# All working tiles of a one-core decoder layer moved by 128 bytes against the weight buffers

## The chip, the cores and the metric

The kernel runs on one core of one Trainium2 chip. The time is the device time of one execution in microseconds (us); smaller is better. Three runs of the kernel before gave 1163.86, 1164.48 and 1166.04 us, median 1164.48.

## The reference

One layer of a decoder trunk on a sequence of 512 tokens with 1024 channels in float32: a half-step FFN, a mixer of two gated linear attention branches, a second half-step FFN, and a last RMSNorm. Shift, scale and gate of each sub-layer come from a vector c.

```python
mod = (cond @ w_ada[l] + b_ada[l]).reshape(b_, N_SUB, 3, d)
h = modulate(rms_norm(x, norm_gains[l, 0]), mod[:, 0, 0], mod[:, 0, 1])
x = x + 0.5 * mod[:, 0, 2][:, None, :] * swiglu(h, ffn1_w_in[l], ffn1_w_down[l])
h = modulate(rms_norm(x, norm_gains[l, 1]), mod[:, 1, 0], mod[:, 1, 1])
proj = h @ w_in_mix[l]
...
merged = (jax.nn.sigmoid(r_hg) * (y_hg @ w_up_hg[l])
          + jax.nn.sigmoid(r_gla) * (y_gla @ w_up_gla[l]))
x = x + mod[:, 1, 2][:, None, :] * (merged @ w_out[l])
h = modulate(rms_norm(x, norm_gains[l, 2]), mod[:, 2, 0], mod[:, 2, 1])
x = x + 0.5 * mod[:, 2, 2][:, None, :] * swiglu(h, ffn2_w_in[l], ffn2_w_down[l])
```

The FFNs have 2816 inner channels; the attention branches (HGRN2 and GLA) have four heads each and are computed in chunks of 64 tokens.

## The kernel before

**Precision.** A float32 product is made of three matmuls in fp32r, which takes one pass: both operands are split into a high part (rounded to fp32r) and a low part (the rest), and high x high, high x low and low x high are added in PSUM (`three`, lines 640 to 645, and the loop in `product`, line 891). So every activation tile exists twice, as in HH and HL, UH and UL, TH and TL, MH and ML, and so does every piece of weights, as WH and WL.

**Weights.** They come as units of 256 output columns and up to eight blocks of 128 rows. SyncE's queue loads a unit into RAW0 or RAW1, ScalarE rounds it into WH0 or WH1 (line 1277), VectorE subtracts (WL0 or WL1, line 1817), and TensorE uses it; two buffers take turns. In the FFNs' input projections, the pairs from the third on are computed by a scheme with seven block products in place of eight (Strassen's): `swiglu_sevens` loops over the pairs, twice 1512 matmuls of 256 columns, all at line 891, from 80 to 257 us and from 851 to 1024 us. VectorE and ScalarE make the combined weights by way of SW, and the combined activations TH and TL once. The other units are matmuls of 512 columns (`unit`, `unit_x`), or of 256 (`first_units`, `last_unit`, and some of the first down projection). In the value units (`unit_v`, lines 688 to 690) the roles are swapped: 128 tokens of HH or HL are the weights and 256 columns of WH or WL move. In the low-rank unit the weights are 16 columns wide. The last unit of the first down projection and of the output projection uses LWH and LWL, which lie in the arena.

**Order.** All engines run programs that were written out by hand with semaphores. The change touches none of them.

**Memory.** SBUF tensors are allocated one after the other, each partition from its start: X, RAW0, RAW1, WH0, WH1, WL0, WL1, S, small constants, and at the end one tensor `arena` of 34928 elements (139712 bytes) of each partition. WH0 lies at 49280, WL0 at 65664; every slice of 128 columns of these starts at 128 modulo 512. All other working tiles are laid over the arena (`place`): HH, HL, UH, UL, TH, TL, MH, ML, LWH, LWL, the attention's tiles, the staging buffers of VectorE and ScalarE, and the destinations of the adaLN weights' loads. Each offset in `place`, and each slice of 128, 256 or 512 tokens in them, is a multiple of 512 bytes, with few small exceptions in the attention. So the moving operands of all wide matmuls start at one address modulo 512, which is that of `base`:

```python
arena = sb("arena", [P, (ARENA + 2 * H_BYTES) // 4 + 112])
base = arena_offset(nc, arena)

def place(name, shape, offset, dt=F32):
    return nc.alloc_sbuf_tensor_at(name, shape, dt, offset=base + offset)
```

The tensor `arena` starts at 88960, which is 384 modulo 512. It has 448 bytes (112 elements) more than its tiles need. `arena_offset` gives the first address from there that is 192 modulo 512: 89280.

Of the kernel before, what the change touches and what calls it, by code (L numbers as in the profile page):

```python
# [23 lines left out]
def trunk_program(nc, x, c, w_ada, b_ada, norm_gains, ffn1_w_in, ffn1_w_down, w_in_mix, w_gk_up, b_gk_up,  # L24
# [48 lines left out]
    with ctx:  # L73
# [35 lines left out]
        ARENA = 106496  # L109
# [4 lines that stand above are left out]
# [2424 lines left out]
def arena_offset(nc, arena):  # L2538

    size = arena.shape[1] * 4  # L2540
    start = (nc.sbuf_base - size) // 32 * 32
    return start + (192 - start) % 512


# [21 lines left out]
```

How the kernel before makes its waits and increments, by code:

```python
        @block.sync  # L405
# [1 line left out]
            def load(n, nslot, dst_cols, src, wait=None):  # L407
                if wait is not None:
                    sp.wait_ge(unit_lo, wait)
                sp.dma_start(dst_cols, src).then_inc(raw_in[nslot], 16)
# [36 lines left out]
            load_pair(0)
            with sp.Fori(1, NP - 1) as i:
                load_pair(i)
            for j in range(11):
                n = N_F1DOWN + j
                kb0, nk = ((0, 8), (8, 8), (16, FB - 16))[j % 3]
                load(n, slot(n), raw(n, nk), cols(ffn1_w_down[0], j // 3 * CW, kb0, nk), n - 1)
                if j == 6:
                    sp.wait_ge(unit_done, 2 * NP)
                    sp.dma_start(LRAW[0][:, :, :], cols(ffn1_w_down[0], 3 * CW, 16, FB - 16)).then_inc(last_in, 16)
            wm = w_in_mix[0]
# [5 lines left out]
            for pair in range(DB // 2):  # L467
                n = N_END + 3 * pair
                load(n, slot(n), raw(n), cols(wm, RHG + CW * pair), n - 1)
                load(n + 1, slot(n + 1), raw(n + 1), cols(wm, RGLA + CW * pair), n)
                up = raw(n + 2)
                sp.wait_ge(unit_lo, n + 1)
                sp.dma_start(up[:, 0:4, :], cols(w_up_hg[0], CW * pair, 0, 4)).then_inc(raw_in[slot(n)], 16)
                sp.dma_start(up[:, 4:8, :], cols(w_up_gla[0], CW * pair, 0, 4)).then_inc(raw_in[slot(n)], 16)
# [14 lines left out]
                sp.dma_start(out[0, t * P:(t + 1) * P, cs], OUTT[:, t, cs]).then_inc(out_dma, 16)  # L489
            sp.wait_ge(fin_a, 2)
            store(0, slice(0, D))
```

## Time and profile before

| | |
|---|---|
| runs, us | 1163.86, 1164.48, 1166.04 |
| profiled execution, us | 1160.54 |
| its span, first to last instruction, us | 1158.5 |
| mean granted TensorE clock | 0.995 of full |
| TensorE busy | 1131.1 us, 98% |
| weight loads busy (they overlap) | 1011.1 us, 87% |
| VectorE, ScalarE, GpSimd busy | 67%, 44%, 9% |
| chain that ended last | TensorE 86%, VectorE 7%, ScalarE 4% |

A matmul's duration in the profile is longer than its distance from the next one, since they are pipelined. Where TensorE never idles, the number of matmuls in a stretch and the distance between their starts say more than the busy share.

### The profile page before, as it was taken

How to read it: one execution, taken by the hardware profiler on the slowest of the kernel's cores; microseconds unless marked ns; L12 is line 12 of the kernel's file. 1: busy time of each engine (PE TensorE's matmuls, PEld its weight loads, DVE VectorE, ACT ScalarE, POOL GpSimd, SP SyncE). 2: the span in 40 equal slices, each digit the busy share in tenths (PEclk: the TensorE clock that was granted, in tenths of full speed). 3: DMA queues.
4: the chain of work that ended last, by engine and by line, in shares of the span. 5: the costliest groups of instructions: out<-in, count | busy, mean ns of one | idle time of the engine just before them, and what ended most of it. 6: DMA issues, size and time to landing. Idle time of an engine off the chain costs nothing.

```text
span 1158.5 us, 18518 instructions
## 1 busy us (share of the span) xinstructions
PE 1131.1 (98%) x7359; PEld 1011.1 (87%) x7359; DVE 778.3 (67%) x1061; ACT 507.2 (44%) x647; POOL 109.4 (9%) x172
## 2 busy tenths in 40 slices
PE   6999999999999999999999999999999999999997
PEld 5789999998889997877887888878999999988887
DVE  4789888867887656567763456855868888863322
ACT  6445544454212465555464321234445545442322
POOL 2000000002221032120210024300000000000000
PEclk9899999999999999999999999999999999999999
DMA  9424333337886222121312457642223333332211
GB/s 351 160 83 135 109 109 107 99 108 246 282 284 217 73 74 73 40 73 42 105 37 74 163 174 245 192 145 73 74 73 109 109 109 109 109 123 85 93 64 73
DMA packets 115799, 144.83 MB, mean 125 GB/s; under 512 B 4420, under 2 KB 103136, under 8 KB 115744
## 3 DMA queue, kind: packets, MB, share of 16 engines
q1 hardware_dynamic: 106800, 113.32, 30.1%
q0 software_dynamic: 8704, 30.68, 7.7%
q8 instruction: 37, 0.61, 0.2%
q14 instruction: 18, 0.15, 0.0%
q10 hardware_dynamic: 240, 0.08, 0.0%
HBM read 140.65 MB, written 2.10 MB: 123 GB/s over the span
## 4 chain that ended last, share of the span: by engine, by line
PE 86%; DVE 7%; ACT 4%; issue 1%; DMA 1%; SPq 0%; DVEq 0%; ACTq 0%
PE PS L891 29%; PE PS L643 16%; PE PS L645 16%; PE PS L644 16%; PE PS L1066 1%; PE PS L688 1%; PE PS L690 1%; PE PS L689 1%; DVE ACC L1919 1%; DMA ADA<-in_w_ada_dram 1%; DVE ACC_FIRSTa L1930 1%; PE PS L970 1%; ACT WH L1277 1%; PE PS L805 1%; DVE ACC_FIRSTb L1930 1%
## 5 line engine op out<-in xcount | busy, mean ns | idle before, releaser
L1817 DVE TENSOR_TENSOR WL<-RAW,WH 128x2048 fp32r<-128x2048 f32 (+2 forms) x55 | 120.5, 2190 | 137.5 <-ACT WH L1277 137.3
L643 PE MATMUL PS<-HH,WH 128*128 128x512 f32 (+2 forms) x488 | 186.6, 382 | 4.3 <-DVE HL L1845 3.2
L1277 ACT ACTIVATE WH<-RAW 128x2048 fp32r<-128x2048 f32 (+2 forms) x55 | 100.5, 1828 | 189.8 <-PE PS L645 181.1
L645 PE MATMUL PS<-HH,WL 128*128 128x512 f32 (+2 forms) x488 | 178.3, 365 | 0.0
L644 PE MATMUL PS<-HL,WH 128*128 128x512 f32 (+2 forms) x488 | 177.8, 364 | 0.0
L891 PE MATMUL PS<-HH,WH 128*128 128x256 f32 x576 | 160.5, 279 | 0.7 <-DVE WL L2107 0.6
L891 PE MATMUL PS<-HH,WL 128*128 128x256 f32 x576 | 159.9, 278 | 0.0
L891 PE MATMUL PS<-HL,WH 128*128 128x256 f32 x576 | 159.9, 278 | 0.0
L643 PE MATMUL PS<-UH,WH 128*128 128x512 f32 (+1 forms) x416 | 146.7, 353 | 0.0
L645 PE MATMUL PS<-UH,WL 128*128 128x512 f32 (+1 forms) x416 | 146.3, 352 | 0.0
L644 PE MATMUL PS<-UL,WH 128*128 128x512 f32 (+1 forms) x416 | 145.6, 350 | 0.0
L891 PE MATMUL PS<-TH,WH 128*128 128x256 f32 x432 | 120.1, 278 | 0.0
L891 PE MATMUL PS<-TH,WL 128*128 128x256 f32 x432 | 119.9, 278 | 0.0
L891 PE MATMUL PS<-TL,WH 128*128 128x256 f32 x432 | 119.9, 278 | 0.0
L643 PEld LDWEIGHTS PS<-HH,WH 128*128 128x128 f32 (+1 forms) x488 | 91.6, 188 | 24.2 <-issue 5.5
L891 PEld LDWEIGHTS PS<-HH,WH 128*128 128x128 f32 x576 | 108.1, 188 | 1.4 <-DVE WL L2107 1.0
L2101 DVE TENSOR_TENSOR WL<-SW,WH 128x1024 fp32r<-128x1024 f32 x72 | 88.1, 1224 | 31.2 <-ACT WH L1460 30.9
L891 PEld LDWEIGHTS PS<-HH,WL 128*128 128x128 f32 x576 | 108.2, 188 | 0.0
L891 PEld LDWEIGHTS PS<-HL,WH 128*128 128x128 f32 x576 | 108.0, 187 | 0.1
L645 PEld LDWEIGHTS PS<-HH,WL 128*128 128x128 f32 (+1 forms) x488 | 91.5, 187 | 16.7
L644 PEld LDWEIGHTS PS<-HL,WH 128*128 128x128 f32 (+1 forms) x488 | 91.8, 188 | 15.2 <-issue 1.3
L1460 ACT ACTIVATE WH<-SW 128x1024 fp32r<-128x1024 f32 x72 | 76.3, 1060 | 63.0 <-PE PS L891 60.1
(345 smaller groups left out, 2219.6 us busy)
## 6 DMA issues: line engine op xcount, KB each, us to landing
RAW<-in_ffn_w_in_dram SPq DMA_DIRECT2D x42, 1024.0 KB, 5.1
ADAW<-in_w_ada_dram POOLq DMA_DIRECT2D x56, 512.0 KB, 6.0
RAW<-in_w_in_mix_dram SPq DMA_DIRECT2D x22, 1024.0 KB, 5.2
RAW<-in_ffn_w_down_dram SPq DMA_DIRECT2D x16, 1024.0 KB, 5.1
ADA<-in_w_ada_dram SPq DMA_DIRECT2D x16, 512.0 KB, 10.5
RAW<-in_ffn_w_down_dram SPq DMA_DIRECT2D x7, 768.0 KB, 5.7
RAW<-in_w_out_dram SPq DMA_DIRECT2D x3, 1024.0 KB, 5.8
XST<-in_x_dram SPq DMA_DIRECT2D x4, 512.0 KB, 5.3
```

The source lines that it names most:

```text
L643: mm(ps, whi, ahi, start=start, stop=False)
L644: mm(ps, whi, alo, start=False, stop=False)
L645: return mm(ps, wlo, ahi, start=False, stop=stop)
L688: mm(ps, HH[:, k, tok], whi[:, k, :], start=k == 0, stop=False)
L689: mm(ps, HL[:, k, tok], whi[:, k, :], start=False, stop=False)
L690: ins = mm(ps, HH[:, k, tok], wlo[:, k, :], start=False, stop=k == DB - 1)
L891: ins = mm(PS[:, bank, ROW], wt, at_tokens[:, k, :], start=start and k == 0 and j == 0, stop=k == 3 and j == 2, skip_group_check=True)
L1277: A(WH[slot(n)][:, 0:size], RAW[slot(n)][:, 0:size], ACT.Copy).then_inc(unit_hi, 1)
L1460: A(WH[tile][:, 8 * P * (1 - j):8 * P * (2 - j)], SW[:, 2 * j:2 * j + 2, :].rearrange("p s c -> p (s c)"), ACT.Copy).then_inc(op_hi, 1)
L1817: V.tensor_tensor(WL[s][:, 0:size], RAW[s][:, 0:size], WH[s][:, 0:size].bitcast(F32), ALU.subtract)\
L1930: V.scalar_tensor_tensor(ACC_FIRST[half][:, :], w, COND[:, k:k + 1], ACC_FIRST[half][:, :], ALU.mult, ALU.add)\
L2101: V.tensor_tensor(WL[tile][:, w], SW[:, 2 * j:2 * j + 2, :].rearrange("p s c -> p (s c)"), WH[tile][:, w].bitcast(F32), ALU.subtract).then ...
```

## The change

The address of the arena's tiles modulo 512 bytes becomes 320 in place of 192. The first such address from 88960 is 89408, so that every tile that `place` lays out lies 128 bytes higher, and the last ends where the tensor `arena` ends. X, RAW, WH, WL, S and the constants stay. The instructions and their order on each engine are the same.

```diff
@@ -2539,7 +2539,7 @@
 
     size = arena.shape[1] * 4
     start = (nc.sbuf_base - size) // 32 * 32
-    return start + (192 - start) % 512
+    return start + (320 - start) % 512
```

## Rows read from the trace of the kernel before

**Rows 1.** The page's parts 1 and 4, of the whole span
```profile
PE 1131.1 (98%) x7359; PEld 1011.1 (87%) x7359; DVE 778.3 (67%) x1061; ACT 507.2 (44%) x647; POOL 109.4 (9%) x172
...
PE 86%; DVE 7%; ACT 4%; issue 1%; DMA 1%; SPq 0%; DVEq 0%; ACTq 0%
```

**Rows 2.** The chain that ended last in order of time: start us, us, what
```profile
95.94 162.41 PE PS L891 x1380
...
862.32 162.49 PE PS L891 x1428
```

**Rows 3.** Busy time by stretch of us from the start; the header names the columns
```profile
core 0: us, PE busy (x) PEld busy (x) DVE busy (x) ACT busy (x) POOL busy (x), PEclk, DMA share, GB/s
44.00:50.00 6.00, 5.49 (x15) 4.37 (x16) 4.90 (x7) 2.97 (x4) 0.00 (x0) 0.59 0.18 62
92.00:105.00 13.00, 12.88 (x114) 12.71 (x113) 12.01 (x17) 7.38 (x12) 0.00 (x0) 1.00 0.48 160
105.00:257.00 152.00, 152.00 (x1293) 152.00 (x1292) 123.94 (x160) 76.31 (x101) 0.00 (x0) 1.00 0.32 104
696.00:767.00 71.00, 71.00 (x308) 57.67 (x308) 47.82 (x53) 18.56 (x13) 23.18 (x35) 1.00 0.71 216
868.00:1024.00 156.00, 156.00 (x1378) 155.91 (x1377) 132.06 (x171) 80.56 (x108) 0.00 (x0) 1.00 0.33 108
```

**Rows 4.** Groups, 106:256, then 870:1023 us; columns: xcount | busy us, mean ns | idle
```profile
L891 PE MATMUL PS<-HH,WH 128*128 128x256 f32 x245 | 68.6, 280 | 0.0
...
L891 PE MATMUL PS<-HH,WH 128*128 128x256 f32 x259 | 71.5, 276 | 0.0
```

**Rows 5.** Timeline of PE, 512 columns, two runs' first and last: start us, us, ...
```profile
747.64 0.40 PE L645 MATMUL PS<-YHh,WL 128*128 128x512 f32 x1
...
750.91 0.40 PE L644 MATMUL PS<-YLh,WH 128*128 128x512 f32 x1
...
1041.13 0.39 PE L643 MATMUL PS<-UH,WH 128*128 128x512 f32 x1
...
1043.19 0.39 PE L643 MATMUL PS<-UH,WH 128*128 128x512 f32 x1
```

**Rows 6.** Timeline of PE, first and last of 26 on LWH and LWL
```profile
791.83 0.28 PE L643 MATMUL PS<-MH,LWH 128*128 128x256 f32 x1
...
794.83 0.28 PE L644 MATMUL PS<-ML,LWH 128*128 128x256 f32 x1
```

**Rows 7.** Groups, whole span; the last row, of line 690, has ns min/median/max
```profile
L643 PE MATMUL PS<-HH,WH 128*128 128x512 f32 x352 | 146.0, 415 | 0.9 <-DVE HL L1953 0.7
...
L643 PE MATMUL PS<-UH,WH 128*128 128x512 f32 x264 | 104.0, 394 | 0.0
...
L643 PE MATMUL PS<-UH,WH 128*128 128x256 f32 x152 | 42.8, 281 | 0.0
...
L644 PE MATMUL PS<-HL,WH 128*128 128x256 f32 x128 | 35.8, 279 | 0.0
...
L645 PE MATMUL PS<-HH,WL 128*16 128x512 f32 x8 | 3.2, 395 | 0.0
...
L690 PE MATMUL PS<-WL,HH x128: 276/281/283, 416.3 to 598.2; 128*128 128x256 f32 x128
```

**Rows 8.** Timeline of all engines about the wait at 397 us
```profile
397.27 0.28 PE L645 MATMUL PS<-HH,WL 128*128 128x256 f32 x1
...
398.28 0.19 PEld L643 LDWEIGHTS PS<-HH,WH 128*128 128x128 f32 x1 [0.93 <-DVE HL L1845]
```

**Rows 9.** Groups by line and form, 397.42:398.26 us, which only this matmul and one before reach
```profile
L645 PE MATMUL PS<-HH,WL 128*128 128x256 f32 x1 | 0.3, 279 | 0.0
```

**Rows 10.** Timeline of PE at the start of the first FFN
```profile
45.93 0.63 PE L643 MATMUL PS<-HH,WH 128*128 128x512 f32 x1
...
48.49 0.59 PE L643 MATMUL PS<-HH,WH 128*128 128x512 f32 x1
```

**Rows 11.** Timeline of PE where the second loop enters the lower level
```profile
868.15 0.36 PE L891 MATMUL PS<-HH,WH 128*128 128x256 f32 x1
```

## The prediction, made before the changed kernel ran

> **What bounds the kernel.** I read the page first, then the groups of matmuls by line and shape, then stretches of the timeline at the resolution of single matmuls. The page says that TensorE is busy for 98% of the span and holds 86% of the chain that ended last [rows 1]; VectorE holds 7% of that chain and the DMAs 1%. Two pieces of the chain are unbroken runs of 1380 and 1428 matmuls of the seven-product loops, 162 us each [rows 2]. So the time is the sum of the distances from one matmul's start to the next one's, and a change that moves no instruction can only act through these distances. The change moves none: it moves addresses. The profiled execution took 1160.54 us around a span of 1158.5; the median of the runs is 1164.48, so 4 us lie between them, and I put my differences on the median.
>
> **What the distances are.** They are not set by the shape alone. In the first seven-product loop (105 to 257 us) 1293 matmuls of 256 columns fill 152.0 us, 117.6 ns each; in the second (868 to 1024 us) 1378 of them fill 156.0 us, 113.2 ns each [rows 3]. The code, the operands' tiles and the granted clock (1.00) are the same. Their durations differ in the same way, 280 ns in the first loop, 276 in the second [rows 4]. The matmuls of 512 columns also have two levels: 9 steps in 2.06 us from 1041.13 (228.9 ns) and 14 steps in 3.27 us from 747.64 (233.6 ns) [rows 5]. I call them the lower and the upper level; they are 4.4 to 4.7 ns apart in both shapes. A third value stands where weights and moving operand both lie in the arena: 25 steps of matmuls on LWH and LWL take 3.00 us, 120.0 ns each [rows 6]. There the two operands start at the same address modulo 512, everywhere else in the main work they start 64 bytes apart, the moving one above; in the value units (lines 688 to 690) HH and HL are the weights and WH and WL move, so the moving one is 64 below.
>
> **What the change does.** The arena goes up by 128 bytes as a whole, from 89,280 to 89,408. (1) Instructions, waits, DMAs and their order: none added, removed or moved, 0 us. (2) Operands that both lie in the arena keep their distance: LWH and LWL, the scores, the VectorE and ScalarE work within it, 0 us. (3) Both old and new start are multiples of 64 and not of 256. The DMAs into the arena keep their size and number; all of them together hold 1% of the chain, some 12 us [rows 1], of which a tenth either way would be 1.2 us, and I take 0 since the pieces keep their size. (4) What is left is the distance between the operands in the wide matmuls, 64 bytes before and 192 now (in the value units 64 below becomes 192 below). With weights of 128 columns no row has this distance, so its price is bounded from both sides.
>
> The counts for these bounds: of the 3024 matmuls at line 891, 1492 lie in the two stretches at the lower level (1378 and 114, [rows 3]), so about 1530 are at the upper. Other matmuls of 256 columns and mean 279 to 281 ns, upper level, are 456 on UH and UL, 384 on HH and HL at lines 643 to 645, and 384 of the value units, of which I take 320 as upper since their shortest is 276 and their median 281 [rows 7]. That makes 2690 upper and 1490 lower. Of 512 columns there are 1056 on HH, HL and 792 on UH, UL [rows 7] and 336 more on the M and Y tiles (three times the 48 and 64 that the code's loops give), 2184 in all; the 308 from 696 to 767 us [rows 3] lie about the run of 233.6 ns and are taken as upper, some 1870 are lower.
>
> Lower bound of the time: all go to the lower level, 2690 x 4.4 ns = 11.8 us and 310 x 4.6 ns = 1.4 us less, 1164.5 - 13.2 = 1151.3. Upper bound: all go to the upper level, 1490 x 4.4 ns = 6.6 us and 1870 x 4.6 ns = 8.6 us more, 1179.7. The price of equal placement is as high: 2690 x 2.4 ns and 1490 x 6.7 ns would be 16.4 us, 1180.9, the wide matmuls not counted.
>
> **Which value I take: zero.** Three things speak against a dependence on the distance of 64 against 192. First, a matmul keeps its level when no weights load beside it. The last one before a wait, from 397.27 us, has the next load only at 398.28 [rows 8], and lasts 279 ns [rows 9], exactly like its neighbours in that upper stretch. If the extra time of a level were a collision of the moving stream with the next weights, this one should have been rid of it. Second, the value units have the moving operand 64 below the weights in place of 64 above, and show the same pair, 276 as the least and 281 as the median [rows 7]. A sign that changes nothing makes it likely that a size that stays clear of zero changes nothing. Third, in the low-rank unit the weights are 16 columns wide and step by 64 bytes with each k, so their distance runs through 64, 0 and on to 192 at k = 6; its matmuls of 512 columns mean 395 ns on line 645 [rows 7], within the two levels of the others, though their loads are short. Against all this stands only the 120.0 ns at distance zero. The second loop enters the lower level about 868.15, where one matmul lasts 0.36 us in place of 0.28 [rows 11], and no operand's placement changes there, so I take the levels as a matter of how the streams fall in step after an interruption. That can fall otherwise in another execution: the profiled execution and the median are 4 us apart with the same addresses, about what one loop's change of level is worth (1293 x 4.4 ns = 5.7 us).
>
> Of the two operands' reads the page's rows say nothing. The Trainium skill ("TensorE: Matmul & The Clock Gate", on the drain phase of a matmul; "SBUF — State Buffer", "SBUF: two separate sides") has moving data and weights read through two independent ports, and says that engines meet only at a port that VectorE and GpSimd share. By that rule the change is worth nothing at any distance. The trace agrees for 64 above and 64 below, and disagrees at distance zero, where 118 has become 120 ns; the sum by the rule is the same 0 as mine.
>
> **The rivals.**
> A, faster: the nearness of 64 bytes is what lets the upper level in, and three times the distance shuts it out. For it: at zero the distance is longest (120.0), at 64 shorter, so farther may be shorter still. Against it: the matmul without a load, and the second loop, which holds the lower level for 156 us at a distance of 64. If the first loop alone turns, 5.7 us go: 1158.8; if all do, 1151.3.
> B, slower: at 192 bytes the two streams meet in the middle of a matmul where at 64 they did not, and the second loop, with all that is now lower, loses its level. The place is 868 to 1024 us and the 512-column units on either side; the price 6.1 us for the loop (1378 x 4.4), 1170.6, and up to 1179.7 with the rest. It decides as soon as more than 520 matmuls turn (520 x 4.4 ns = 2.3 us, 0.2%). For it: the lower level holds in only about half the work, so it is easily lost; against it, the same three things as for my forecast.
> C, much faster: everything above the bare stream goes. At the lower of the clock's two levels, 1.2 GHz (granted 0.59 over 44 to 50 us, [rows 3]), six matmuls of 512 columns take 2.56 us, 427 ns each [rows 10]; half of it is 213.5 ns against 229 at 2.4 GHz, and 106.7 for 256 columns. That would be 15.5 x 1870 + 20 x 310 ns for the wide ones and 11 x 2690 + 6.5 x 1490 ns for the others, some 74 us, 1090. Nothing but arithmetic is for it.
> D, it does not do what it says: ruled out by the allocation, since 448 spare bytes of the arena are exactly what the new start needs, and every tile in it moves alike.
>
> **How the numbers follow.** No dependence on the distance: 0.45, and the median then lies within 1161 to 1168, since it can still fall in step otherwise. A 0.28, B 0.25, C 0.02. A measurement tells about 0.2% (2.3 us) from nothing. Of the 0.45 I give 0.37 to the same time and 0.04 to either side, so faster 0.34, same 0.37, slower 0.29. The time is that of the likeliest case, 1164.0, half a microsecond below the median because the profiled execution was 4 us below it. The range takes in A nearly to its end and B to its end, 1152 to 1179, and leaves C out.
>
> **What would show it.** Right: the second loop again near 113 ns a matmul and the first near 118, or the two changed about with the same sum; LWH still 120; the value units with least 276. A is right if no stretch of 256 columns shows 279 or more. B is right if the second loop's mean duration is 279 or more and fewer than 1340 matmuls lie in 156 us. I am wrong at the root if a duration appears that before does not have, below 276 or above 283 ns for 256 columns outside LWH, or outside 388 to 398 ns for 512, in an unbroken run: then the distance enters the price itself and not the level.

## The result and the profile after

The changed kernel takes 1170.32 us, the median of 4 runs (1169.38 to 1172.32), against 1164.65 of the kernel before (1163.86 to 1166.04, 4 runs). The ratio is 1.0042 with a 95% interval of 1.0025 to 1.006: slower by 0.4%, 5.7 us. The profiled execution is one of the four, 1169.64 us, with a span of 1167.6. Of all runs reported here one, of the kernel with the arena at 160, took 1878.43 us at a granted clock of 0.56; it is left out.

The page's parts 1 and 4 of the changed kernel, the same lines as [rows 1]:
```profile
PE 1140.5 (98%) x7359; PEld 1014.1 (87%) x7359; DVE 779.5 (67%) x1061; ACT 508.1 (44%) x647; POOL 110.1 (9%) x172
...
PE 88%; DVE 6%; ACT 3%; issue 1%; DMA 1%; SPq 0%; DVEq 0%; ACTq 0%
```
The counts are those of before; TensorE is busy for 9.4 us more in a span that is 9.1 longer. In the chain of waits the first loop's piece is as long as in [rows 2], the second's 5.8 us longer (start us, us, what):
```profile
94.47 162.77 PE PS L891 x1380
...
864.33 168.26 PE PS L891 x1428
```
The stretches of [rows 3], the columns as there:
```profile
44.00:50.00 6.00, 5.28 (x23) 4.31 (x24) 5.11 (x7) 3.19 (x4) 0.00 (x0) 1.00 0.30 104
92.00:105.00 13.00, 12.88 (x110) 12.71 (x110) 11.22 (x17) 8.09 (x12) 0.00 (x0) 1.00 0.39 130
105.00:257.00 152.00, 152.00 (x1293) 152.00 (x1292) 123.40 (x159) 75.24 (x100) 0.00 (x0) 1.00 0.32 104
696.00:767.00 71.00, 71.00 (x310) 57.34 (x309) 49.61 (x52) 19.10 (x14) 23.74 (x35) 1.00 0.68 208
868.00:1024.00 156.00, 156.00 (x1329) 155.91 (x1328) 131.12 (x170) 79.25 (x105) 0.00 (x0) 1.00 0.32 105
```
The first loop still holds 1293 matmuls in 152 us. The second holds 1329 in place of 1378 in 156 us: it is at the upper level now, and the granted clock is 1.00 in both. The groups of the two loops over the same stretches as in [rows 4], first and second, say the same by their durations:
```profile
L891 PE MATMUL PS<-HH,WH 128*128 128x256 f32 x244 | 68.6, 281 | 0.0
...
L891 PE MATMUL PS<-HH,WH 128*128 128x256 f32 x251 | 70.5, 281 | 0.0
```
The matmuls of 512 columns, where [rows 5] had 228.9 ns in the last down-projection, in the timeline of TensorE (the first and the last of 23):
```profile
1047.83 0.39 PE L643 MATMUL PS<-UH,WH 128*128 128x512 f32 x1
...
1052.97 0.39 PE L644 MATMUL PS<-UL,WH 128*128 128x512 f32 x1
```
That is 22 steps in 5.14 us, 233.6 ns each. LWH and LWL, which keep their distance of zero, keep their price of [rows 6] (first and last of 36):
```profile
794.76 0.28 PE L643 MATMUL PS<-MH,LWH 128*128 128x256 f32 x1
...
798.95 0.28 PE L645 MATMUL PS<-MH,LWL 128*128 128x256 f32 x1
```
35 steps in 4.19 us are 119.7 ns. Last, the groups that answer to [rows 7], of the whole span:
```profile
L643 PE MATMUL PS<-UH,WH 128*128 128x512 f32 x264 | 105.1, 398 | 0.0
...
L643 PE MATMUL PS<-UH,WH 128*128 128x256 f32 x152 | 42.9, 282 | 0.0
...
L690 PE MATMUL PS<-WL,HH x128: 277/279/283, 416.0 to 598.4; 128*128 128x256 f32 x128
```
The 512-column group is 4 ns longer; the 256-column ones stay within the old pair of durations.

A trace gives the start of every matmul, so the span can be added up by shape. The table shows the sum of the distances to the next start in us and, for the steady ones, the mean in ns; "interrupted" are distances of over 266 ns, in waits or at the low clock of the opening (for 256 columns, over 138 ns, not shown). The loops are counted from their thirteenth matmul; "other 256" leaves LWH and LWL out. The columns before and after come from the profiles above; the two on the right are the first pair of experiments, the same two programs again.

| | before | after | before again | after again |
|---|---|---|---|---|
| profiled execution | 1160.54 | 1169.64 | 1166.83 | 1172.98 |
| 512 columns, steady | 2116: 486.4 (229.9) | 2127: 496.2 (233.3) | 2115: 486.0 (229.8) | 2128: 496.4 (233.3) |
| 512, interrupted | 92: 39.6 | 81: 33.0 | 93: 39.9 | 80: 32.9 |
| first loop | 175.6 (117.4) | 175.7 (117.4) | 175.9 (117.6) | 176.0 (117.7) |
| second loop | 170.1 (113.7) | 175.5 (117.3) | 175.8 (117.5) | 175.3 (117.2) |
| other 256, steady | 143.3 (117.5) | 141.2 (116.1) | 143.3 (117.5) | 142.0 (116.7) |

The first pair's 9.1 us come from two large parts: the steady 512-column matmuls, (233.3 - 229.9) x 2127 = 7.2 us, and the second loop, 5.4 us. Against them, "other 256" is 2.1 us shorter, and by its 200th matmul (at 52 us) the kernel after is 1.8 us ahead. The medians are only 5.7 us apart: the profiled execution of before was 3.3 us below the fastest of its four runs.

### The profile page after: what moved, and what is told of

The parts are those of the page before. It is cut to its first block, busy times and chain, and to the rows that moved or that the text cites. A ratio compares the mean times of both kernels' runs of the same rounds, so it can differ in the third digit from the quotient of the medians.

```text
span 1167.6 us, 18518 instructions
## 1 busy us (share of the span) xinstructions
PE 1140.5 (98%) x7359; PEld 1014.1 (87%) x7359; DVE 779.5 (67%) x1061; ACT 508.1 (44%) x647; POOL 110.1 (9%) x172
## 4 chain that ended last, share of the span: by engine, by line
PE 88%; DVE 6%; ACT 3%; issue 1%; DMA 1%; SPq 0%; DVEq 0%; ACTq 0%
PE PS L891 29%; PE PS L643 17%; PE PS L645 16%; PE PS L644 16%; PE PS L1066 1%; PE PS L688 1%; PE PS L690 1%; PE PS L689 1%; DVE ACC L1919 1%; DMA ADA<-in_w_ada_dram 1%; DVE ACC_FIRSTa L1930 1%; PE PS L970 1%; ACT WH L1277 1%; PE PS L805 1%; PE PS L976 1%
```

## The experiments

After the result I had two theories. **Distance**: the price of a matmul depends on how far the moving operand's start lies from the weights', 64 bytes against 192, and the second loop's change of level is part of it. **Own address**: it depends on where the arena itself lies modulo 512 (320 against 192). A third was that the whole loss is the second loop and **chance**. Sixteen runs follow, of fourteen new kernels and the two again. All times are medians in us, with the range and the number of runs. Five chips were used; each ratio is to runs of the kernel before on the same chip in the same hour, so it is the ratios that compare across kernels.

**The two programs again.** No edit.

> The kernel before, unchanged, for a second profile. Theory D (distance): the time of the wide matmuls hangs on how far the moving operand starts from the weights, modulo 512. Then the 512-column runs stand at 229 ns again as they did in the first profile (outside 696 to 767 us), whatever the 256-column loops do. Theory C (chance): both shapes fall into a level by chance after each interruption. Then the 512-column runs change their level against the first profile in some stretches of hundreds of matmuls. Both expect 1164 to 1166 us; for the two seven-product loops I expect that the level can differ from the first profile, 113 or 118 ns.

> The changed kernel, for a second profile. Theory D (distance): 512-column runs at 233.4 ns throughout, as in its first profile, 1169 to 1172 us. Theory C (chance): runs at 229 ns appear in some stretches, and the time scatters toward 1165.

Before again 1166.61 (1164.38 to 1167.26, 10 runs), ratio to the other runs of before 1.0004 (0.9994 to 1.0014). After again 1172.91 (1171.89 to 1173.6, 4), 1.0055 (1.0037 to 1.0073). The stretches from 868 us and the opening, of before again:
```profile
44.00:50.00 6.00, 5.29 (x15) 4.15 (x15) 5.17 (x7) 3.23 (x4) 0.00 (x0) 0.57 0.21 73
868.00:1024.00 156.00, 156.00 (x1329) 155.90 (x1328) 129.68 (x168) 78.12 (x104) 0.00 (x0) 1.00 0.32 105
```
and of after again:
```profile
44.00:50.00 6.00, 4.56 (x21) 3.48 (x22) 5.15 (x9) 2.84 (x5) 0.00 (x0) 1.00 0.54 175
868.00:1024.00 156.00, 155.89 (x1329) 155.72 (x1328) 131.83 (x172) 79.09 (x106) 0.00 (x0) 1.00 0.33 108
```
The second loop holds 1329 matmuls in both: with the old addresses, too, it can run at the upper level. Its 5.4 us in the first pair of profiles are chance and not the change's; the table's two right columns have both loops alike and still differ by 6.15 us. What differs between the old and the new addresses in all four traces is the steady 512-column matmul, here 229.8 against 233.3 ns: 3.5 x 2128 = 7.4 us.

The opening differs also: after again begins its unbroken matmuls of 512 columns at 47.4 us with the full clock, before again at 44.8 with the granted clock at 0.57, so that it starts 2.6 us later and has about a dozen matmuls less at 427 ns (12 x 0.2 = 2.4 us back). By the 200th matmul it is 0.7 us behind. The lateness, too, goes with the granted clock, which was low at another place: from 21.9 to 25.6 us it is 0.50 in after again and 1.00 in before again.
```profile
21.90:25.60 3.70, 3.63 (x17) 3.63 (x18) 0.02 (x1) 1.40 (x2) 0.00 (x0) 0.50 1.04 384
...
21.90:25.60 3.70, 3.70 (x34) 3.70 (x35) 1.77 (x4) 2.40 (x5) 0.00 (x0) 1.00 1.05 383
```
The addresses don't decide it: in the profile of after, with the addresses of after again, the unbroken matmuls start at 44.7, with the full clock. With 7.4 us for the 512 columns, 0.7 for the opening, and 1.3 and 0.4 less for the other 256-column matmuls and the loops, the sum is 6.4 of the 6.15 us.

"Other 256" is shorter in both pairs, by 2.1 and 1.3 us, and at least one stretch of it goes with the addresses: 96 matmuls from about 1117 us take 117.8 ns in the three traces where all operands are 64 bytes apart (before, before again, and the kernel at 320 below) and 113.4 ns in the four where they are 192 apart (after, after again, and the kernels at 448 and at 64 below). So the level that a short stretch of 256 columns takes isn't only chance. In the second loop both distances show both levels (the lower in before and in the kernel at 64); the first loop is at the upper one in all seven.

**The distance or the arena's own address.** All weights and with them what lies behind go up by 128 bytes; the arena goes to 320 (distance 64 again) or to 448 (distance 192).
```diff
+        PAD = sb("PAD", [P, 32])
         WH = [sb(f"WH{s}", [P, UNIT], F32R) for s in range(2)]
...
-    return start + (192 - start) % 512
+    return start + (448 - start) % 512
```

> Arena at 320 as in the change, but the weight buffers moved up by 128 bytes too (256 modulo 512), so that the distance is 64 again. Theory D (distance between the operands): 512-column runs back at 229 ns, time 1163 to 1167 us. Theory A (the moving operand's own address decides): 233.4 ns and 1169 to 1172 us, as with the change.

> Weight buffers at 256 and arena at 448 modulo 512: distance 192 as in the change, at other addresses. Theory D (distance): 233.4 ns for 512 columns, 1169 to 1172 us. Theory A (own address): a value of its own, most likely 229 ns and 1165 us if only 320 was unlucky.

At 320: 1164.44 (1157.59 to 1167.05, 10), ratio 0.9979 (0.996 to 0.9999). At 448: 1166.03 (1157.73 to 1172.36, 10), 0.9988 (0.9961 to 1.0015). The timeline of the one at 448 in the last down-projection (first and last of 23):
```profile
1050.76 0.39 PE L645 MATMUL PS<-UL,WH 128*128 128x512 f32 x1
...
1055.89 0.39 PE L646 MATMUL PS<-UH,WL 128*128 128x512 f32 x1
```
22 steps in 5.13 us, 233.2 ns. The one at 320 (first and last of 23) has 22 steps in 5.04 us, 229.1 ns, and a mean of 229.8 over all its steady ones:
```profile
1048.06 0.39 PE L645 MATMUL PS<-UL,WH 128*128 128x512 f32 x1
...
1053.10 0.39 PE L646 MATMUL PS<-UH,WL 128*128 128x512 f32 x1
```
An arena at 320, the changed kernel's own place, has the old price as soon as the weights have moved along, and one at 448, the old place modulo 256, has the new price: own address falls, distance stands. The times are too scattered to say it. Ten runs at 448 lie 15 us apart, within what the 4200 matmuls of 256 columns are worth between their two levels (4.4 ns x 4200 = 18.5 us), and their median is that of before. So with this chance in it a median of a few runs is weak evidence, that of the result's four included, and the steady distances in the trace are the measure from here on.

**Other distances, by the arena alone.** Only the constant of the last line changes, to 64, 128, 160, 224, 256, 288, 352 and 384; the one at 352 also takes 32 bytes more of spare arena.
```diff
-    return start + (192 - start) % 512
+    return start + (128 - start) % 512
```

> Arena at 64 modulo 512: the moving operand starts 64 bytes below the weights (448 above, modulo 512). Theory R256 (what counts is the distance modulo 256, 192 and -64 being the same): 512-column runs at 233.4 ns, LWH unchanged at 120, time 1169 to 1173 us. Theory N (nearness, whatever the sign): 229 ns and 1164 to 1167 us as at +64. The 256-column loops fall in either level in both.

> Arena at 128: distance zero for all wide matmuls, as LWH and LWL have. Theory Z (zero is dear): all 256-column runs at 120 ns in place of 113 to 118, which is 4200 x 2.4 to 6.7 ns, 10 to 28 us more, and the 512-column runs above 233: 1175 to 1200 us. Theory L (the 120 of LWH comes from its order of use and not from its place): 113 or 118 ns as elsewhere and 1163 to 1173 us.

> Arena at 160: distance 32. So far 256-column runs cost 120.0 ns at distance 0 and 256, 113.3 or 117.75 at 64 and 192, 118.7 on average at 128; 512-column runs 226.8, 229.0 (64), 233.3 (192), 232.4 (128). Theory R256 (a smooth course with a period of 256): between 0 and 64, 227 to 229 ns for 512 columns and 117 to 120 for 256, time 1166 to 1172 us. Theory G (64 is what the memory is cut into): 32 behaves as one of its neighbours exactly.

> Arena at 224: distance 96. Theory R256: between 64 and 128, 229 to 232.4 ns for 512 columns, 116 to 119 for 256, 1166 to 1175 us. Theory G: exactly as 64 or exactly as 128.

> Arena at 256: distance 128. Theory N (nearer is better down to 64): between the two, 229 to 233 ns for 512 columns and 1165 to 1171 us. Theory R128 (0 and 128 are alike): as with the arena at 128, 120 ns and up.

> Arena at 288: distance 160, which is -96. If the sign does not matter (32 as -32 and so on): as distance 96, 233.3 ns and 120.0 ns, 1181 us. If it does: a value of its own between those of 128 and 192, 232 to 233 ns and 113 to 119 ns, 1170 to 1175 us.

> Arena at 352 (with 32 bytes more of spare room): distance 224, which is -32. If the sign does not matter: as distance 32, 233.3 ns and 116.7 ns, 1168 to 1172 us. If it does: between 192 and 0, 227 to 233 ns and 113 to 120 ns.

> Arena at 384: distance 256, half of 512. Theory N: no better than 192, 233.4 ns, 1169 to 1173 us. Theory R256: as distance zero, so as with the arena at 128 whatever that gives.

The steady distances, worked out from the starts of the matmuls in each trace, with the times. "Distance" is the moving operand's start less the weights', modulo 256; the kernels before and after are among them. The columns in ns give what the long unbroken stretches show, for 256 columns the two loops; the mean over all steady 512-column matmuls is 227.6 at distance zero and 229.8 at 64, and within 0.2 ns of the table's elsewhere.

| arena | distance | 512 columns, ns | 256 columns, ns | median (range, runs) | ratio (95%) |
|---|---|---|---|---|---|
| 128 | 0 | 226.8 | 120.0 | 1171.62 (1171.56–1172.07, 5) | 1.0039 (1.0025–1.0053) |
| 384 | 256 = 0 | 226.8 | 120.0 | 1171.26 (1168.3–1171.88, 6) | 1.0031 (1.0019–1.0044) |
| 160 | 32 | 233.3 | 116.7 | 1169.88 (1167.44–1172.27, 9) | 1.0042 (1.0019–1.0065) |
| 192, before | 64 | 229.0, a fifth 233.3 | 113.3 or 117.75 | 1166.61 (1164.38–1167.26, 10) | 1.0004 (0.9994–1.0014) |
| 224 | 96 | 233.3 | 120.0 | 1181.62 (1181.5–1181.7, 4) | 1.0144 (1.0106–1.0182) |
| 256 | 128 | 232.4 | 118.7 | 1175.18 (1173.32–1176.48, 4) | 1.0064 (1.0047–1.0081) |
| 288 | 160 | 234.3 | 118.7 | 1176.89 (1176.36–1178.85, 4) | 1.0097 (1.008–1.0114) |
| 320, after | 192 | 233.3 | 113.3 or 117.75 | 1172.91 (1171.89–1173.6, 4) | 1.0055 (1.0037–1.0073) |
| 64 | 192 | 233.3 | 113.3 or 117.75 | 1166.99 (1160.45–1172.99, 10) | 1.0001 (0.9971–1.0032) |
| 352 | 224 | 233.3 | 118.3 | 1175.22 (1174.98–1175.81, 4) | 1.0083 (1.0066–1.01) |

To see the two shapes apart, the stretches 120 to 250 us (256 columns) and 640 to 690 us (mostly 512) of before again:
```profile
120.00:250.00 130.00, 130.00 (x1106) 130.00 (x1105) 108.60 (x140) 64.43 (x86) 0.00 (x0) 1.00 0.33 106
640.00:690.00 50.00, 50.00 (x220) 41.01 (x219) 21.53 (x19) 14.41 (x11) 9.18 (x14) 1.00 0.59 195
```
of the one at 128 (distance zero):
```profile
120.00:250.00 130.00, 130.00 (x1086) 130.00 (x1085) 106.29 (x139) 64.14 (x86) 0.00 (x0) 1.00 0.32 105
640.00:690.00 50.00, 50.00 (x220) 41.07 (x219) 23.79 (x20) 17.95 (x15) 7.98 (x12) 1.00 0.53 178
```
and of the one at 224:
```profile
120.00:250.00 130.00, 130.00 (x1085) 130.00 (x1085) 106.29 (x140) 64.36 (x86) 0.00 (x0) 1.00 0.31 105
640.00:690.00 50.00, 50.00 (x214) 39.88 (x214) 23.07 (x21) 19.36 (x17) 7.97 (x12) 1.00 0.48 162
```
The matmul counts beside PE read 1106, 1086 and 1085 in 130 us of the loop. (At 640 us the kernels are not all at the same place in the program, so that the 220, 220 and 214 tell less than the steady distances do.) The two programs at distance zero have the same pair of prices although their arenas lie 256 bytes apart, and so have 320 and 64: the distance counts modulo 256. It has no symmetry otherwise, 32 is not 224 and 96 is not 160. The loops at 64 and at 192 have the same pair of levels, while the 512 columns have different prices. And the two shapes want different distances: zero is the cheapest for 512 columns and, with 96, the dearest for 256. That was not expected of any: for zero I had put the 512 columns above 233, and for 32 and 96 values between their neighbours.

The value units give the same finding inside single traces, since their operands change roles and their distance is the negative one. With the arena at 160 they are at 224 and take 118.3 ns, where the loops of that trace take 116.7; at 352 they are at 32 and take 116.7 to 116.8 (one stretch 117.8), where the loops take 118.3; at 288 they are at 96 and take 119.8 to 120.0. Outside the loops some placements show a second level as well: 117.3 to 117.5 beside 118.7 at 160, 120.0 beside 118.7 at 128. For 512 columns at 64, the fifth at 233.3 stands mostly between 696 and 767 us, and at the same places in all three traces. At 96, where both are dear, the kernel loses 1.4%: (233.3 - 229.8) x 2128 = 7.4 us and, against 117.6, 2.4 ns x some 4200 = 10 us, together 17.5, where 15 to 17 were measured. The arena at 64 shows how much the levels can hide: it has the distance and the prices of the changed kernel, and the median of before. Three of its ten runs lie at 1160.5 to 1160.9, three at 1164.8 to 1167.1 and four at 1172.3 to 1173.0, and the profiled one has its second loop at the lower level.

**The 512-column matmuls alone.** If they carry the whole loss, a kernel that changes the distance for them and leaves the 256-column ones at 64 must show it. The weights' buffers get 128 (or 64) bytes more, with small constants between them so that each still starts at 128 modulo 256, and units of 512 columns are written and read that much higher in their buffer:
```diff
+        def at_unit(tiles, n):
+            o = 32 if wide(n) else 0
+            return tiles[slot(n)][:, o:o + UNIT]
...
-                hi = WH[slot(n)][:, :].rearrange("p (k c) -> p k c", c=width)
-                lo = WL[slot(n)][:, :].rearrange("p (k c) -> p k c", c=width)
+                hi = at_unit(WH, n).rearrange("p (k c) -> p k c", c=width)
+                lo = at_unit(WL, n).rearrange("p (k c) -> p k c", c=width)
```
With 32 elements their distance becomes 64 - 128, which is 192 modulo 256; with 16 elements it becomes zero. In the first two kernels some units of the down-projections are still written at the buffer's start and read 128 or 64 bytes beside it, so that these products take wrong weights, at the addresses described; the third computes all of it.

> Arena at 192 as before; only the units whose matmuls have 512 columns get their weights 128 bytes higher in the weight buffers, so that their distance is -64, which is 192 modulo 256; the 256-column units keep 64. If the wide matmuls carry the loss: 233.3 ns for them, some 7 us over the kernel before, 1171 to 1174 us, as with the change. If the loss needs the 256-column matmuls too: less than half of it, under 1169 us.

> The same with 64 bytes in place of 128: distance 0 for the 512-column matmuls, 64 for the others. If each width pays by its own distance: 226.8 ns for 2184 matmuls of 512 columns against 229 to 233 (mean 229.9), 6.8 us less than before, 1158 to 1161 us, and 113.3 or 117.75 ns for the 256-column loops as before. If a mix brings costs at the seams or from the shifted buffers: no gain, 1164 us and more.

> Distance 0 for all units whose matmuls have 512 columns, 64 for the 256-column ones, the whole computation as in the reference. As for mix0: 226.8 ns in the 512-column runs, 1158 to 1162 us, ratio to the kernel before 0.995 to 0.998. If the gain of mix0 came from the units that it read beside their place: no gain.

At distance 192 for the wide ones alone: 1172.29 (1172.13 to 1173.05, 4), ratio 1.0058 (1.0041 to 1.0075), the changed kernel's loss and within a us its time. Its stretches:
```profile
120.00:250.00 130.00, 130.00 (x1106) 130.00 (x1106) 108.34 (x141) 65.02 (x87) 0.00 (x0) 1.00 0.32 105
640.00:690.00 50.00, 50.00 (x216) 40.30 (x215) 23.10 (x19) 15.90 (x14) 8.54 (x13) 1.00 0.56 184
```
The loop is that of before again, 1106; the 512-column stretch holds 216 in place of 220, and the mean over the steady ones is 233.2 ns. At distance zero for the wide ones: 1161.91 (1160.12 to 1162.79, 6), 0.9969 (0.9955 to 0.9982). The timeline of the full one, first and last of 23:
```profile
1039.83 0.39 PE L657 MATMUL PS<-UL,WH 128*128 128x512 f32 x1
...
1044.82 0.39 PE L658 MATMUL PS<-UH,WL 128*128 128x512 f32 x1
```
22 steps in 4.99 us are 226.8 ns; the mean over its 2126 steady ones is 227.5, against 229.8. The full kernel takes 1161.61 (1159.41 to 1162.18, 12 runs), but before in that hour took 1160.64 (1158.21 to 1166.99, 17 runs, in clusters about 1158, 1161, 1164 and 1167), so the ratio is 0.9996 (0.9978 to 1.0014). Its 512-column matmuls are worth 2.3 x 2126 = 4.9 us, and they are in its trace: it has both loops at the upper level (175.6 and 176.2 us), as before again has, both are at 54.0 us by their 200th matmul, and its span is 5.0 us shorter (1159.7 against 1164.7). A faster kernel by the medians I can't claim. That before had its loops at the lower level more often in that hour would explain it, but no trace of those runs was kept, so it isn't shown. The spread between the two mixed kernels is clear: 1172.29 against 1161.91, 10.4 us, for the distance of the wide matmuls alone.

**Do the two weight tensors count apart?** The 128 bytes only before WL: products with WH keep the distance 64, those with WL get 192.
```diff
         WH = [sb(f"WH{s}", [P, UNIT], F32R) for s in range(2)]
+        PAD = sb("PAD", [P, 32])
         WL = [sb(f"WL{s}", [P, UNIT], F32R) for s in range(2)]
```

> Only the low weights WL moved up by 128 bytes, WH and the arena as before: distance 64 for two of three matmuls and 192 for the third. Theory L1 (each matmul pays for its own pair, or for the weights that load beside it): a third of the 512-column matmuls at about 233 ns and the rest at 229, mean 230.4, 1167 to 1169 us. Theory L2 (the level is one state of the whole run, set by any of its pairs): all of them at 233.3 or all at 229.

1166.61 (1163.06 to 1173.56, 10), ratio 1.003 (1.0003 to 1.0057). Among the 512-column matmuls on the attention output's tiles the steps that begin with MH on WH take 234.7 ns, ML on WH 235.1 to 235.3, MH on WL 229.8 to 230.2; in before again they take 232, 226 to 229 and 229 to 231. So the steps that begin with a matmul at distance 64 have become dear, and the one that begins at 192 is not: the price of a matmul is not that of the distance to its own weights alone, the neighbours' count too. By stretch, the units at 258 us keep 229.0 and the last down-projection from 1025 us is at 233.3, mean over all 232.1; the first loop stands at 118.9 ns and the second at 113.3. So neither of my two theories came. A pattern for single pairs I did not get out of it.

## Why the prediction was wrong

I forecast 1164.0 within 1152 to 1179 and no difference as the likeliest; the time is 1170.3, inside the range, and the kernel is slower. Point by point:

*TensorE's chain bounds the kernel, and only distances between starts can change.* Right, but for the opening, which moved by about 2 us with the granted clock. Instructions and the share of the DMAs are as before.

*Edits (1) and (2) at 0 us.* Right for what is seen: LWH's price stayed at 119.7 to 120.0 ns.

*(3), the DMAs into the arena, at 0.* Nothing in the page speaks against it (DMA holds 1% of the chain as before); no run measures it by itself.

*(4), the distance: the value taken, zero.* This step failed, and mainly for one of the two shapes. For the 256-column matmuls of the loops it holds: at distance 64 and at 192 they show the same two levels, and which one the second takes differs between executions, as I wrote; shorter stretches gained 1.3 to 2.1 us in all. For the 512-column ones the distance decides: at 64 four fifths take 229.0 ns and the rest 233.3, at the same places each time, and at 192 all take 233.3. The term stood in my upper bound, 1870 x 4.6 ns = 8.6 us; it measured 3.4 ns x 2127 = 7.2 us, less because more of them were above 229.0 before than the 310 I had counted, and the step is 4.3 ns and not 4.6.

*Two kinds of level taken for one.* That is why I missed it. I saw 228.9 and 233.6 ns beside 113.2 and 117.6, 4.4 to 4.7 apart in both shapes, called both the lower and upper level, took both for chance after an interruption, and argued for both from one of them. All three arguments came from elsewhere: the matmul without a load beside it has 256 columns, and so have the value units. My sign argument held (the value units at 64 below are at 192 modulo 256 and show the pair of 64 above, which is what 256 columns do), but it said nothing of 512. The third, the low-rank unit's 16-column weights, has 512 columns but short loads, and its mean of 395 ns on line 645 I read as between the levels; after the change it is 393. The table by shape that I made afterwards could have been made before: it would have shown two shapes with two behaviours.

The rule cited from the Trainium skill ("TensorE: Matmul & The Clock Gate" on the drain phase; "SBUF — State Buffer", "SBUF: two separate sides"), that moving data and weights come through two independent read ports, gives 0 us at every distance. The runs disagree: 226.8 to 234.3 ns for 512 columns and, by loop, 113.3 to 120.0 for 256, for the same instructions at a granted clock of 1.00.

*Rival B, slower, 1170.6 by the second loop.* The sign, the time and even its signs in the profile came (281 ns, 1329 in 156 us), and its mechanism is not what cost the time: before again has the same 1329. The agreement of 1170.6 with 1170.3 is luck. B's "up to 1179.7 with the rest" named the 512-column units, and they are the cause. *Rival A* has only the short stretches for it: the first loop stayed at 1293. *Rival C*, the bare stream of 213.5 and 106.7 ns: the best seen at any distance are 226.8 and 113.3. *D*: the change did what it says.

*"Wrong at the root if a duration appears that before does not have."* This sign misled too: the durations stayed within 388 to 398 ns, since every price that came with the change was one that before already showed somewhere. What changed was how many matmuls have it.

What stays open: why 64, 192 and the rest modulo 256 have these prices; what decides the 256-column level after an interruption; and why the neighbours' distances count. Distances that aren't multiples of 32 bytes were not tried, as the tiles are placed in steps of 32.

## What to carry to other kernels

In a kernel that is one long run of matmuls, the steady distance between starts is to be tabulated by shape before any theory: one shape's levels may be chance while another's are set by addresses. Where the moving operand starts relative to the weights modulo 256 bytes is worth up to 3% of a 512-column matmul and up to 6% of a 256-column one, and the best place differs by shape. So an arena is to be placed by the sum over the shapes of the number of matmuls times the difference in price, and not by the shape that has the most time: here that would be the 512 columns (2200 x 230 against 4200 x 117 ns), and their best place, zero, gains 2200 x 2.3 ns = 5 us on them and loses 4200 x 2.4 = 10 on the others; it measured 0.3 to 0.4% slower. Giving each shape its own offset in the weight buffers avoids the choice. When single executions scatter by several us for a reason that is known, the count of matmuls in a fixed stretch without idle time tells what ten runs' median doesn't.

## What the hardware showed that I had not expected

The price of a matmul depends on the two operands' distance modulo 256, separately for each shape: 512 columns 226.8 (0), 229.0 with a fifth at 233.3 (64), 232.4 (128) and 233.3 to 234.3 ns elsewhere; 256 columns, in the loops, 116.7 (32), 113.3 or 117.75 (64, 192), 118.3 to 118.7 (128, 160, 224), 120.0 (0, 96). It is the sign and size of the distance modulo 256 that counts: operands moved together keep the price, and units whose operands change roles have the price of the negative distance.

At 64 and 192 the 256-column matmuls hold one of two spacings, 4.4 ns apart, through nearly a whole loop (in before's second from 868 us to its end), and the same program takes either one in another execution (170.1 and 175.8 us for the second loop of before). Of the arenas whose loops show a single spacing three repeat within 0.2 to 0.8 us (224, 128, 352) and four within 2.5 to 4.8 (288, 256, 384, 160); those with the pair range from 1.7 us (after again, 4 runs) to 14.6 (the one at 448 with moved weights, 10 runs).
